# Hybrid layer with a 32-expert MoE: residual and final norm through PSUM, a first pair without scatter, and w_in's first block ahead of x

## The reference, cut to what matters

```python
h = rmsnorm(x, g_mix);  proj = h @ w_in            # 1024 x 2048
x = x + concat(y_pool, y_attn) @ w_out
h2 = rmsnorm(x, g_ffn)
top_vals, top_idx = top_k(h2 @ w_router + b_router, 4)   # 4 of 32 experts
for e in range(32):
    gu = h2 @ w_gu[e] + b_gu[e]                    # w_gu[e]: 1024 x 2048
    gate, lin = min(gu[:, :1024], 7), clip(gu[:, 1024:], -7, 7)
    y = (gate * sigmoid(1.702 * gate) * (lin + 1)) @ w_down[e] + b_down[e]
    out += combine[:, e] * y                       # combine: softmax weight or 0
x = x + out
return rmsnorm(x, g_final)
```

## Time and profile before

| What | Value |
|---|---|
| three runs, median (lowest to highest) | 1038.88 us (1036.74 to 1042.88) |
| profiled execution, its own time | 1037.48 us |
| its span, first to last instruction | 1034.8 us |
| TensorE matmul busy | 956.8 us (92%) |
| VectorE, ScalarE, GpSimd busy | 284.8, 133.7, 18.2 us |
| DMA | 419.41 MB, mean 405 GB/s |
| chain that ended last, by engine | PE 53%, DMA 41%, DVE 4% |
| granted TensorE clock, mean | 0.996 |

### The profile page before, as it was taken

One profiled execution on the slowest core, in us unless ns is written; L12 is line 12 of the kernel. 1 busy time (PEld: TensorE's weight loads), 2 busy tenths in 40 slices (PEclk: granted clock), 3 DMA queues, 4 the chain that ended last, 5 costly groups with the idle time before them and its releaser, 6 DMA issues.

```text
span 1034.8 us, 12029 instructions
## 1 busy us (share of the span) xinstructions
PE 956.8 (92%) x4841; PEld 427.4 (41%) x4841; DVE 284.8 (28%) x537; ACT 133.7 (13%) x200; POOL 18.2 (2%) x20
## 2 busy tenths in 40 slices
PE   7999999999999989989899999989898999989895
PEld 7988443434343333434243243434343343424331
DVE  6954331222221213122121213113121312213113
ACT  7634001010100000000000000000000000000102
POOL 0500000000000000000000000000000000000000
PEclk9999999999999999999999999999999999999999
DMA  9569899999999999999999999999999999999993
GB/s 359 205 261 396 343 380 415 428 428 430 429 426 429 429 429 428 430 429 426 429 429 429 428 430 429 426 429 429 428 428 430 429 426 429 429 428 428 428 427 146
DMA packets 34489, 419.41 MB, mean 405 GB/s; under 512 B 5300, under 2 KB 5960, under 8 KB 9864
## 3 DMA queue, kind: packets, MB, share of 16 engines
q1 hardware_dynamic: 34432, 419.16, 96.1%
q10 hardware_dynamic: 40, 0.01, 0.0%
HBM read 418.10 MB, written 1.05 MB: 405 GB/s over the span
## 4 chain that ended last, share of the span: by engine, by line
PE 53%; DMA 41%; DVE 4%; issue 1%; ACT 0%; SPq 0%; ACTq 0%; DVEq 0%
PE ps L909 50%; DMA raw<-in_w_down 37%; DMA raw<-in_w_gu 3%; PE ps L1142 2%; DVE woutl L653 1%; DVE xT L750 1%; DMA win<-in_w_in 1%; PE ps L1193 0%; ACT sm L477 0%; PE ps L998 0%; DVE mxs L670 0%; DVE sm L665 0%; PE ps L1166 0%; DVE outs L900 0%; PE ps L1052 0%
## 5 line engine op out<-in xcount | busy, mean ns | idle before, releaser
L909 PE MATMUL ps<-raw,xT 128*64 128x512 f32 x2048 | 459.6, 597 | 23.1 <-DMA raw<-in_w_gu 22.8
L909 PEld LDWEIGHTS ps<-raw,xT 128*64 128x64 f32 x2048 | 140.9, 137 | 322.0 <-issue 265.1
L909 PE MATMUL ps<-raw,actT 128*64 128x512 f32 x1024 | 233.4, 597 | 24.6 <-DMA raw<-in_w_down 24.6
L909 PEld LDWEIGHTS ps<-raw,actT 128*64 128x64 f32 x1024 | 72.2, 136 | 161.2 <-issue 147.4
L840 DVE TENSOR_TENSOR biased<-ps,biasT 128x1024 f32<-128x1024 f32 x32 | 39.2, 1224 | 335.5 <-PE ps L1142 335.5
L541 ACT ACTIVATE gu<-ps 128x1024 f32<-128x1024 f32 x32 | 32.8, 1024 | 527.8 <-PE ps L909 527.8
L857 DVE TENSOR_TENSOR acc<-ps,acc 128x512 f32<-128x512 f32 x64 | 41.2, 686 | 135.4 <-PE ps L909 135.4
L750 DVE TENSOR_TENSOR xT<-ps,gT 128x512 f32<-128x512 f32 x32 | 22.1, 691 | 180.1 <-PE ps L909 180.1
L909 PE MATMUL ps<-ysc,dispT 64*128 64x512 f32 x272 | 67.8, 615 | 0.8 <-DVE ysc L891 0.8
L909 PEld LDWEIGHTS ps<-disp,h 128*128 128x128 f32 x512 | 61.6, 196 | 12.4 <-issue 12.2
L909 PE MATMUL ps<-disp,h 128*128 128x128 f32 x512 | 64.8, 285 | 0.2 <-DVE disp L744 0.2
(11 more groups left out here) (163 smaller groups left out, 428.6 us busy)
## 6 DMA issues: line engine op xcount, KB each, us to landing
raw<-in_w_gu SPq DMA_DIRECT2D x128, 2048.0 KB, 32.6
raw<-in_w_down SPq DMA_DIRECT2D x64, 2048.0 KB, 34.7
win<-in_w_in SPq DMA_DIRECT2D x16, 512.0 KB, 12.5
wout<-in_w_out SPq DMA_DIRECT2D x4, 1024.0 KB, 9.4
acc<-in_x SPq DMA_DIRECT2D x2, 512.0 KB, 3.8
out<-outs SPq DMA_DIRECT2D x2, 512.0 KB, 3.1
gfin<-in_g_final SPq DMA_DIRECT2D x1, 512.0 KB, 9.5
cst<-in_consts SPq DMA_DIRECT2D x1, 402.0 KB, 7.7
```

Of the source, the lines that this page charges most:

```text
L909: return pe.matmul(out_, lhsT, rhs, start=start, stop=stop, skip_group_check=shared)
```

## The change

Seven things are altered.

1. SP issues w_in's block 0 ahead of x and the constants after block 2; ScalarE and VectorE take block 0 before the first piece of turned x.
2. Pair 0 is taken out of the loops on all engines and has no scatter and no adds. The loops start at pair 1 on ScalarE and VectorE, and at the third pair on TensorE.
3. The down biases have a tile of their own (`bdown`), are loaded after g_final, and the turned combine weights stay in `combT`. The scatter of pair 14, which runs in the last pair, starts each bank with a product of `combT` and `bdown` over 32 rows.
4. In the last pair TensorE brings `acc` into four banks by products with the identity (`residual_in`): two after chunk 5 of the gate/up, one after chunk 6, one ahead of the last expert's down unit 0.
5. The last down load is two transfers (`load_pieces`), and the last down unit is cut in two with `last_scatter(0, 0)` before it and `last_scatter(0, 1)` between its halves. Its outputs go to bank 6.
6. The adds of the end go. ScalarE squares and VectorE multiplies by g_final straight from PSUM, in turn on the two banks of a tile. There is one inverse and one root for both tiles. SP stores tile 0, then tile 1. GpSimd no longer takes part.
7. The copy of the top indices to float goes; the compare reads the integers.

```diff
+bdown = at("bdown", [P, 512], F32, 132 * KB)
+combT = at("combT", [P, TT, P], F32, 134 * KB)
...
+FINAL = ((0, 1), (5, 7))
+Y_LAST = 6
...
-    for t in range(TT):
-        sp.dma_start(acc[:, t, :], x[0, t * P:(t + 1) * P, :]).then_inc(x_loaded[t], 16)
     for h in range(2):
         for c in range(DC):
             sp.dma_start(win[:, h, c, :], w_in[0, c * P:(c + 1) * P, h * HALF:(h + 1) * HALF]).then_inc(
                 win_loaded[h][c], 16)
-            if h == 0 and c == 1:
+            if h == 0 and c == 0:
+                for t in range(TT):
+                    sp.dma_start(acc[:, t, :], x[0, t * P:(t + 1) * P, :]).then_inc(x_loaded[t], 16)
+            if h == 0 and c == 2:
                 sp.dma_start(cst[:, P:N_CONST], consts[:, P:N_CONST]).then_inc(const_loaded, 16)
...
+    def load_pieces(e, s):
+
+        rows = w_down[0, bass.ds(e, 1), 4 * P:8 * P, :].rearrange("a (p r) n -> p (a r) n", r=4)
+        for v in range(2):
+            sp.dma_start(raw[:, PLACE[s], v, :].rearrange("p (r n) -> p r n", r=2),
+                         rows[:, 2 * v:2 * v + 2, :]).then_inc(piece_loaded[v], 16)
...
-    sp.wait_ge(ysc_zeroed, 1)
-    for h in range(2):
-        sp.dma_start(ysc[h * SLOTS:h * SLOTS + E, 0, :], b_down[0, :, h * 512:(h + 1) * 512]).then_inc(bdown_loaded, 16)
...
+    for h in range(2):
+        sp.dma_start(bdown[h * SLOTS:h * SLOTS + E, :], b_down[0, :, h * 512:(h + 1) * 512]).then_inc(bdown_loaded, 16)
...
+            elif last and k == ITER_U - 1:
+                load_pieces(a + 1, s)
...
-    for t in (1, 0):
+    for t in range(TT):
         sp.wait_ge(out_ready[t], 1)
         sp.dma_start(out[0, t * P:(t + 1) * P, :], outs[:, t, :]).then_inc(stored, 16)
...
-    pool.wait_ge(attended, 2)
-    pool.memset(ysc[:, 0, :], 0.0).then_inc(ysc_zeroed, 1)
     pool.wait_ge(projected, 3)
     pool.memset(comb2[:], 0.0).then_inc(comb2_zeroed, 1)
-    pool.memset(dispT[:, 1, :, :], 0.0).then_inc(dispT_zeroed, 1)
-    pool.wait_ge(scaled, TT)
-    pool.memset(ysc[:, 1, :], 0.0).then_inc(ysc_zeroed, 1)
-    pool.wait_ge(rounds_ready, 1)
-    last_pair = pool.snap(pool.value_load(further[0:1, 0:1], min_val=0, max_val=T // SLOTS - 1) * PAIRS + (PAIRS - 1))
-    pool.wait_ge(gfin_loaded, 16)
-    pool.wait_ge(added, last_pair * 4 + 6 + TT)
-    pool.tensor_tensor(outs[:, 0, :], acc[:, 0, :], gfin[:], ALU.mult).then_inc(out_weighted, 1)
...
+    win_part(0, 0)
     turned_high(0)
-    win_part(0, 0)
...
-            act.activation(ysc[0:SLOTS, 1, :], ps[0:SLOTS, Y[1], :], ACT.Copy).then_inc(outputs_ready, 1)
-
-    with act.Fori(0, last_pair) as i:
+            act.activation(ysc[0:SLOTS, 1, :], ps[0:SLOTS, Y_LAST, :], ACT.Copy).then_inc(outputs_ready, 1)
+
+    iteration(0, False)
+    with act.Fori(1, last_pair) as i:
...
     for t in range(TT):
-        act.wait_ge(added, last_pair * 4 + 6 + TT + 2 * t)
-        act.activation(junk3[t][:], acc[:, t, :], ACT.Square, accum_out=ssq[:, t:t + 1]).then_inc(squares, 1)
-    for t in range(TT):
-        act.wait_ge(inv_ready, 4 + t)
-        act.activation(rs[:, t:t + 1], inv[:, t:t + 1], ACT.Sqrt).then_inc(rstd_ready, 1)
+        act.wait_ge(scattered, last_pair * 4 + (2 + 2 * t))
+        for h in range(2):
+            if h == 1:
+                act.wait_ge(final_weighted, 2 * t + 1)
+            act.activation(junk3[:, t, h, :], ps[:, FINAL[t][h], :], ACT.Square,
+                           accum_out=ssqf[:, t, h:h + 1]).then_inc(final_squared, 1)
+    act.wait_ge(inv_ready, 4)
+    act.activation(rs[:], inv[:], ACT.Sqrt).then_inc(rstd_ready, 1)
     act.wait_ge(rstd_ready, 4)
-    act.wait_ge(out_weighted, 1)
+    act.wait_ge(final_weighted, 2)
     act.activation(outs[:, 0, :], outs[:, 0, :], ACT.Copy, scale=rs[:, 0:1]).then_inc(out_ready[0], 1)
...
+    win_rest(0, 0)
     turned_low(0)
-    win_rest(0, 0)
...
-        link(dve.tensor_copy(i4[:, t, :], i8[:, t, 0:K]))
         link(dve.tensor_tensor(onehot[:, t], bc(c_("experts").rearrange("p (a e) -> p a e", a=1), P, K, E),
-                               bc(i4[:, t, :].rearrange("p (k a) -> p k a", a=1), P, K, E), ALU.is_equal))
+                               bc(i8[:, t, 0:K].rearrange("p (k a) -> p k a", a=1), P, K, E), ALU.is_equal))
...
-    dve.wait_ge(dispT_zeroed, 1)
-    dve.tensor_copy(dispT[:, 0, :, :], ps[:, 4, 0:T].rearrange("p (t q) -> p t q", t=TT)).then_inc(outputs_ready, 1)
+    dve.tensor_copy(combT[:], ps[:, 4, 0:T].rearrange("p (t q) -> p t q", t=TT)).then_inc(combT_ready, 1)
...
-        for job in range(4):
-            add_scattered(i, job)
+        if not isinstance(i, int):
+            for job in range(4):
+                add_scattered(i, job)
...
-    with dve.Fori(0, last_pair) as i:
+    iteration(0, False)
+    with dve.Fori(1, last_pair) as i:
         iteration(i, False)
...
-    dve.wait_ge(scattered, last_pair * 4 + 4)
-    dve.tensor_copy(ysc[SLOTS:P, 1, :], ps[SLOTS:P, Y[1], :]).then_inc(outputs_ready, 1)
-    for job in range(4):
-
-        dve.wait_ge(scattered, last_pair * 4 + job + 5)
-        part = acc[:, job // 2, (job % 2) * 512:(job % 2 + 1) * 512]
-        dve.tensor_tensor(part, ps[:, job, :], part, ALU.add).then_inc(added, 1)
+    dve.wait_ge(scattered, last_pair * 4)
+    dve.tensor_copy(ysc[SLOTS:P, 1, :], ps[SLOTS:P, Y_LAST, :]).then_inc(outputs_ready, 1)
     dve.wait_ge(gfin_loaded, 16)
-    inverse_tile(0, 2 * TT + 1)
-    dve.wait_ge(added, last_pair * 4 + 8 + TT)
-    link(dve.tensor_tensor(outs[:, 1, :], acc[:, 1, :], gfin[:], ALU.mult))
-    inverse_tile(1, 2 * TT + 2)
-    dve.wait_ge(rstd_ready, 5)
+    for t in range(TT):
+        dve.wait_ge(scattered, last_pair * 4 + (2 + 2 * t))
+        for h in (1, 0):
+            if h == 0:
+                dve.wait_ge(final_squared, 2 * t + 1)
+            dve.tensor_tensor(outs[:, t, h * 512:(h + 1) * 512], ps[:, FINAL[t][h], :],
+                              gfin[:, h * 512:(h + 1) * 512], ALU.mult).then_inc(final_weighted, 1)
+    dve.wait_ge(final_squared, 4)
+    link(dve.tensor_tensor(inv[:], ssqf[:, :, 0], ssqf[:, :, 1], ALU.add))
+    link(dve.tensor_scalar(inv[:], inv[:], 1.0 / D, EPS, ALU.mult, ALU.add))
+    dve.reciprocal(inv[:], inv[:]).then_inc(inv_ready, 1)
+    dve.wait_ge(rstd_ready, 4)
+    dve.wait_ge(final_weighted, 4)
     dve.tensor_scalar(outs[:, 1, :], outs[:, 1, :], rs[:, 1:2], None, ALU.mult).then_inc(out_ready[1], 1)
...
+    def down_rows(half, u, s, rows, bank):
+        for r in rows:
             m = 4 * u + r
             for h in range(2):
                 col = r % 2 * D + h * 512
-                ins = mm(ps[h * SLOTS:(h + 1) * SLOTS, Y[half], :], actT[:, half, m, :],
+                ins = mm(ps[h * SLOTS:(h + 1) * SLOTS, bank, :], actT[:, half, m, :],
                          raw[:, PLACE[s], r // 2, col:col + 512], start=m == 0, stop=m == DC - 1)
...
-    def scatter(t):
+    def scatter(t, last):
         for h in range(2):
-            rows = slice(h * SLOTS, (h + 1) * SLOTS)
+            rows, biases = slice(h * SLOTS, (h + 1) * SLOTS), slice(h * SLOTS, h * SLOTS + E)
+            if last:
+                mm(ps[:, M[h], :], combT[biases, t, :], bdown[biases, :], stop=False)
             for a in range(2):
-                ins = mm(ps[:, M[h], :], dispT[rows, a, t, :], ysc[rows, a, :], start=a == 0, stop=a == 1)
+                ins = mm(ps[:, M[h], :], dispT[rows, a, t, :], ysc[rows, a, :],
+                         start=a == 0 and not last, stop=a == 1)
             ins.then_inc(scattered, 1)
...
-    pe.wait_ge(bdown_loaded, 32)
-    pe.wait_ge(ysc_zeroed, 2)
-    pe.wait_ge(dispT_zeroed, 1)
...
-                pe.wait_ge(outputs_ready, i * 2 + 1)
                 pe.wait_ge(gate_clipped, i * 2 + 1)
                 pe.wait_ge(up_clipped, i * 2 + 1)
-                scatter(0)
-            if k == 2:
-                pe.wait_ge(added, i * 4 + TT + 2)
-                scatter(1)
+            if k == 1 and not first:
+                pe.wait_ge(outputs_ready, i * 2)
+                if last:
+                    pe.wait_ge(bdown_loaded, 32)
+                    pe.wait_ge(combT_ready, 1)
+                scatter(0, last)
+            if k == 2 and not first:
+                pe.wait_ge(added, i * 4 - 4 + (TT + 2))
+                scatter(1, last)
             if k == 3:
...
+                if not first:
+                    pe.wait_ge(added, i * 4 - 4 + (TT + 3))
...
+            if k == 5 and last:
+                pe.wait_ge(added, i * 4 - 4 + (TT + 4))
+                residual_in(0, 0)
+                residual_in(0, 1)
+            if k == 6 and last:
+                residual_in(1, 0)
...
-        pe.wait_ge(act_ready, i * 2 + 2)
-        for u in range(DN_U):
-            down_unit(1, u, *unit(j, half, 10 + u - gap))
-            if u == 0 and not last:
-                pe.wait_ge(gate_clipped, i * 2 + 2)
-                pe.wait_ge(up_clipped, i * 2 + 2)
-                turn_gu(i * 2 + 2)
-            if u == 0 and last:
```

(101 more changed lines are left out.)

7 lines of the change are left out of this document (3 added, 4 removed).

## The result

The changed kernel takes 1048.65 us in the median of 7 executions (1044.99 to 1053.03), the kernel before 1039.35 us (7 executions). The ratio is 1.0093 with a 95% interval of 1.0071 to 1.0115: 9.3 us slower, where the forecast was 1036.4 us in a range up to 1039.8. The profiled execution took 1052.01 us, its span 1050.2 us, at a mean granted clock of 0.988 against 0.996 before. Of all executions reported here one stands apart, 1660.45 us in bias64 at a mean granted clock of 0.557, and no ratio or comparison takes it in.

A forecast was written before the change was run, and what follows sets the result against it. The prediction took TensorE as the bound before about 166 us, then the weight stream; -3.8 (pair 0) -0.2 (start) +3.5 (last pair) -1.2 (tail) = -1.7 us from 1038.2 gave 1036.4 us, range 1032.8 to 1039.8.

The forecast's parts named there:

- The step that failed: Last pair: four added bias products, sized at 0.48 us each by a scatter product, cost 1.9 us.
- The rival on the slow side: Last pair: drains at bias and residual products cost more than all is worth; 9.6 us added gives 1040.4; chance 0.12.
- Pair 0: Dropping pair 0's two scatters at 1.92 us each moves later loads 3.84 us sooner; gain 3.8 us, bounds 3.3 and 5.7.
- Both holes: Early weight stream: gaps of 3.3 us and about 1 us, expected to close, the second perhaps only nearly.
- The start: Kernel start: w_in's block 0 ahead of x lets TensorE start 0.2 us sooner.
- the late bound of 8.5: Kernel start: the late case for x's landing, at 8.5 us, with TensorE starting 0.5 us later.
- the bound of 0.5: Kernel start: TensorE starts at most 0.5 us later, if x lands at 8.5 us.
- The residual products: Last pair: four full-array products of 512 columns at about 0.9 us each add 3.6 us; sign 0.86 to 0.9 each.
- The split: Last down load and unit: the split transfer buys nothing; two more shape changes cost about 0.2 us.
- The tail: Kernel end: ScalarE and VectorE working from PSUM in turn bring the first store sooner; gain 1.2 us, bounds 0.6 and 1.6.
- The index copy and the moved bias loads: Routing and prologue: the dropped 0.43 us copy gains nothing, and the two moved b_down issues cost nothing.

The follow-up runs named there:

- bias64: The changed kernel with its four bias products in place but over 64 zero-padded rows, the shape of the scatter products; 1040.34 us, ratio 1.0004 to the kernel before.
- grouped: The changed kernel with both halves' 32-row bias products together ahead of the four scatter products; 1038.72 us, ratio 0.9988 to the kernel before.
- moved: The changed kernel with biases together ahead of the scatter products, in pair 14's own order, and x ahead of w_in; 1036.22 us, ratio 0.9973 to the kernel before.
- interleaved14: The best kernel (pair 0 without scatter, biases in pair 14, old start and end) with each bias ahead of its own half's scatter products; 1036.37 us, ratio 0.9996.
- x_first: The changed kernel with x ahead of w_in's first block again on SP, ScalarE and VectorE; 1047.33 us, ratio 1.0068 to the kernel before.

## Why the prediction was wrong

**The step that failed** is in the last pair: a bias product was sized by the nearest row, a scatter product at 1.92 / 4 = 0.48 us, four of them 1.9 us, with 0.1 to 0.2 us for a change of shape. The four added 8.0 us at the full clock, because 0.48 us is the price of a product that overlaps with the other half's, and the change of shape between the halves ends that. The row could have told it: 0.48 us is half of what a full pass of 512 columns takes (0.9 by the earlier trace rows), so the overlap was in it. The rival on the slow side had the place and the mechanism, but priced a change at 0.2 us and the products at 0.9 at most, 7.4 us over the slack, where the profile shows 10.2 at the full clock and 16.8 with its drops; it was given 0.12. So its 1040.4 us was low by the same step.

**What no step held** is the clock. In the profiled execution it costs 6.6 us in the last pair. The seven executions order by it: 1044.99 and 1046.23 us at a mean granted clock of 0.994, 1047.98 at 0.993, 1048.65 at 0.990, 1052.0 and 1052.1 at 0.988, 1053.03 at 0.987. Half a clock for 14.7 us lowers the mean of 1050 us by 0.007 and costs 7.4 us, close to the 8.0 us between the ends. My estimate for the kernel without the drops of its last pair is about 1045 us, 5.6 us slower than before: that is what the two executions at 0.994 take, and 0.994 is also the mean of grouped's profile, which has early drops but none in its last pair.

**Pair 0** was right: 3.8 us forecast, the load 4.0 us sooner, and the kernel that keeps this and the moved biases alone 4.0 to 4.4 us faster (0.9962 and 0.9958). Both holes closed.

**The start** was on the wrong side: 0.2 us sooner forecast, 1.2 us later in the profile and 1.0 to 1.9 us in the means and medians. x landed at 8.75 us, past the late bound of 8.5; with the 3.0 us that the prediction allowed for its turning that gives 11.75, and the slower turning adds the other 0.4 us, for which the bound of 0.5 us had no place.

**The residual products** took 1.92 + 1.06 + 1.06 = 4.0 us, 3.6 forecast: single ones came out above the 0.86 to 0.9 us named as a sign. **The split** gained nothing, as forecast, and cost 0.35 us instead of 0.2. **The tail** gave 1.5 us instead of 1.2. **The index copy and the moved bias loads** cost or gained nothing visible.

With the 8.0 us in the place of 1.9, 4.0 for 3.6, 0.35 for 0.2, a start of +1.9 and a tail of -1.5, the same sum gives -4.0 + 1.9 + (8.0 + 4.0 + 0.35 - 2.16) - 1.5 = +6.6 us, or +5.7 with a start of +1.0. The 2.7 to 3.6 us up to the measured 9.3 are what is left for the drops of the clock in a median execution; that share was not measured by itself.

A kernel that beats both came out of the runs: pair 0 without scatter, the biases grouped in pair 14, and start and end as before, 1034.65 and 1034.89 us in two sets of runs.

## What to carry to other kernels

In this kernel products that use half of the array's rows were cheap only while the other half's stood next to them in the same shape. Before a product of another shape is put among them, ask what it separates; group the odd shapes at one end. And added work belongs where the wait is long: grouped, the four bias products add 2.1 us to the last pair, whose 2.16 us of slack the residual products have used up; one pair earlier TensorE still waits 1.33 and 1.24 us for loads after them (profile of moved).

## What the runs showed that was not expected

The granted clock fell to 1.2 GHz while TensorE was busy without a gap, for 6 to 7 us at a time, in the last pair of the two profiled kernels with the interleaved scatter there (992 to 998 and 1002 to 1009 us; 998 to 1004 us), and in none of the profiled kernels without it. The mean clocks of single executions say the same: below 0.990 lie three of seven of the changed kernel and three of ten of interleaved14, none of six of x_first, none of the 90 of the kernels with another order, the one of 0.557 aside, and none of the 84 of the kernel before that were timed beside them. Why this order goes with the drops is not shown. One or two drops of about 3.4 us in the first 130 us come in every profile, the kernel before's included (122 to 125 us), at places that differ: between 9 and 16, 100 and 105, and 121 and 130 us.

TensorE turned x by the same 16 instructions in anything from 1.97 to 3.65 us at a granted clock of 1.00, and in at least 3.25 us in the four of these kernels where it had idled 1.9 to 2.7 us before. The first 16 instructions of every profile, behind the idle start, are as slow, 3.52 us in the kernel before and 3.79 in the one after.
